# An expert layer whose rows are gathered by selection products and whose weights pass a ring of 19 slots

## What is computed

```python
h = h + swa_sink_attention(rmsnorm(h), ...);  h = h + swiglu(rmsnorm(h), ffn_w_gu, ffn_w_down)
h = h + mamba2_ssd(rmsnorm(h), ...);          h = h + moe_swiglu(rmsnorm(h), w_router, w_gu, w_down)
return rmsnorm(h, ln_final)

def moe_swiglu(h, w_router, w_gu, w_down):
    logits = h @ w_router
    top_v, top_i = lax.top_k(logits, 2)
    gates = softmax(top_v)                       # two gates a token
    for e in range(8):                           # w_gu[e]: 1024 x 7168, w_down[e]: 3584 x 1024
        g, u = split(h @ w_gu[e]);  out += combine[:, e] * ((silu(g) * u) @ w_down[e])
```

## Time and profile before

| | us |
|---|---|
| median of three executions | 1410.24 (1409.48 to 1411.64) |
| profiled execution, its time | 1411.03 |
| profiled execution, its span | 1409.2 |
| attention to router (0 to 561.3) | 561.3 |
| eight expert passes (561.3 to 1395) | 83.7, 118.0, 95.7, 117.1, 97.9, 116.0, 115.3, 90.0 |
| behind the last expert product | 14.2 |

### The profile page before, as it was taken

The page is one execution under the profiler, slowest core; times in us unless marked ns, Lnnn a source line. Parts: engine busy times, 40 slices in busy tenths (PEclk is TensorE's granted clock), DMA queues, the critical chain, the costliest instruction groups (busy, mean ns, idle before and its releaser), DMA issues.

```text
span 1409.2 us, 30487 instructions
## 1 busy us (share of the span) xinstructions
PE 1348.5 (96%) x13282; PEld 806.3 (57%) x13282; DVE 448.3 (32%) x684; ACT 380.0 (27%) x568; POOL 68.9 (5%) x119
## 2 busy tenths in 40 slices
PE   8999999999999999999999988999988999999985
PEld 7778888887999987353344243345233345346342
DVE  7775555447689974101001000000000000000102
ACT  6754444336588843000000000000000001000011
POOL 2043000000002220100000000000000000000000
PEclk9999999999999999999999999999999999999998
DMA  9369855564643448999999999999999999999994
GB/s 352 125 207 413 302 194 179 180 201 128 209 120 122 150 186 335 374 419 425 415 419 424 412 420 424 412 419 424 414 420 425 413 413 424 414 413 412 404 420 184
DMA packets 130491, 463.07 MB, mean 329 GB/s; under 512 B 9600, under 2 KB 35472, under 8 KB 113984
## 3 DMA queue, kind: packets, MB, share of 16 engines
q1 hardware_dynamic: 123808, 440.44, 79.5%
q0 software_dynamic: 4960, 15.95, 2.9%
q10 hardware_dynamic: 1600, 4.82, 1.1%
HBM read 445.06 MB, written 16.12 MB: 327 GB/s over the span
## 4 chain that ended last, share of the span: by engine, by line
PE 64%; issue 12%; SPq 9%; DMA 9%; DVE 3%; POOLq 2%; ACT 1%; DVEq 1%; POOL 0%; ACTq 0%
PE bank L1332 27%; PE bank L1350 11%; SPq L376 9%; PE bank L826 7%; PE bank L828 7%; PE bank L827 7%; DMA e_ring<-moe_w_gu_in 5%; DMA e_ring<-moe_w_down_in 3%; PE bank L1308 2%; POOLq L477 1%; DMA ring<-swa_w_qkv_in 1%; DVE w_lo L1470 1%; PE bank L1323 1%; POOLq L475 0%; PE bank L1048 0%
## 5 line engine op out<-in xcount | busy, mean ns | idle before, releaser
L1332 PE MATMUL bank<-e_ring,xgT 128*32 128x512 f32 (+1 forms) x4800 | 465.3, 540 | 10.6 <-DMA e_ring<-moe_w_gu_in 10.5
L1332 PEld LDWEIGHTS bank<-e_ring,xgT 128*32 128x32 f32 x4800 | 151.3, 110 | 313.1 <-issue 277.4
L1470 DVE TENSOR_TENSOR w_lo<-ring,w_hi 128x2048 fp32r<-128x2048 f32 (+1 forms) x84 | 191.9, 2288 | 108.9 <-ACT w_hi L520 108.6
L520 ACT ACTIVATE w_hi<-ring 128x2048 fp32r<-128x2048 f32 (+1 forms) x84 | 158.9, 1895 | 126.8 <-PE bank L828 118.7
L1350 PE MATMUL bank<-e_ring,m_hT_a 128*32 128x256 f32 x2240 | 133.8, 396 | 14.3 <-DMA e_ring<-moe_w_down_in 14.3
L2027 DVE TENSOR_TENSOR m_hh<-m_sg,bank 128x512 f32<-128x512 f32 (+1 forms) x40 | 22.7, 616 | 376.1 <-PE bank L1332 376.1
L826 PE MATMUL bank<-w_hi,hT_hi 128*128 128x512 f32 (+1 forms) x336 | 130.9, 390 | 2.2 <-DVE w_lo L1470 1.9
L828 PE MATMUL bank<-w_hi,hT_lo 128*128 128x512 f32 (+1 forms) x336 | 129.2, 385 | 0.0
L827 PE MATMUL bank<-w_lo,hT_hi 128*128 128x512 f32 (+1 forms) x336 | 129.2, 384 | 0.0
L1350 PE MATMUL bank<-e_ring,m_hT_b 128*32 128x256 f32 x1920 | 108.2, 380 | 12.8 <-DMA e_ring<-moe_w_down_in 12.8
L1350 PEld LDWEIGHTS bank<-e_ring,m_hT_a 128*32 128x32 f32 x2240 | 76.4, 114 | 68.0 <-issue 23.1
(11 more groups left out here) (362 smaller groups left out, 1357.8 us busy)
## 6 DMA issues: line engine op xcount, KB each, us to landing
e_ring<-moe_w_gu_in SPq DMA_DIRECT2D x120, 1024.0 KB, 22.0
e_ring<-moe_w_gu_in SPq DMA_DIRECT2D x120, 768.0 KB, 21.6
e_ring<-moe_w_down_in SPq DMA_DIRECT2D x88, 1024.0 KB, 18.6
ring<-ffn_w_gu_in SPq DMA_DIRECT2D x28, 1024.0 KB, 6.3
e_ring<-moe_w_down_in SPq DMA_DIRECT2D x32, 512.0 KB, 15.3
ring<-ffn_w_down_in SPq DMA_DIRECT2D x14, 1024.0 KB, 4.9
xg_rows<-zeros POOLq DMA_DIRECT2D x48, 256.0 KB, 16.3
ring<-ssm_w_in_in SPq DMA_DIRECT2D x8, 1024.0 KB, 5.0
```

Source lines behind the costliest of these rows:

```text
L520: act.activation(w_hi[:, m % SPLIT, 0:w], ring[:, m % RING, 0:w], ACT.Copy).then_inc(hi_ready, 1)
L1332: ins = pe.matmul(bank[banks[b]][quad, 0:w], xgT[:, k, rows], e_slot(c)[:, block_n * w:(block_n + 1) * w], start=(k == 0), stop=(k == KD - ...
L1470: dve.tensor_tensor(w_lo[:, m % SPLIT, 0:w], ring[:, m % RING, 0:w], w_hi[:, m % SPLIT, 0:w].bitcast(F32), ALU.subtract).then_inc(lo_ready, 1)
```

## The change

- **Ring.** 19 slots: `e_late` holds two slots where `e_last` was one; `e_top` holds two behind the tensors of the layers, in space gained by setting the scratch that POOL's DMA descriptors use to 2048 bytes a partition. Loads ahead of the experts are 19: two right behind the stream (`c_dt_parts`), two behind `SO0`, one behind `c_y`, six behind `lo_ready`, one behind `c_norm`, six behind `chunk_used`, one behind `r_mm`. Chunks 16, 17 and 18, the additional ones, are of 768 KB.
- **Loads in line.** SP's loop is over rounds; the 365 loads behind the first 19 of a round are written out.
- **Rows.** `xg_rows`, its zeros, the scatter, the row loads, `rows_T`, `spread` and the DVE comparisons of `shares_of` go. `xs` stays resident. In each pass DVE makes `sel` (which token goes to which row of the next pass) and `gated` (the same for the own pass, times the gate) (`selections`, `pass_sel`); PE multiplies `gated` by the identity (`pass_shares`, 4 products) and `xs` by `sel` (`rows_next`, 16 products); DVE copies the former into `shares_T`. PE waits for `rows_ready` before the first pass.
- **Small loads.** `rw` and `dtw` are loaded by ACT (in its early list, before `ahead(2)`) instead of by POOL.
- The rows of pass 0 are gathered 64 wide instead of 96.

```diff
@@ ring
-ERING = 16
-SLOT_OF = (13, 14, 15, 0, 1, 2, 3, 4, 5, 6, 7, 8, 9, 10, 11, 12)
+CONTIGUOUS = 15
+SLOT_OF = (17, 18, 13, 14, 15, 0, 1, 2, 3, 4, 5, 16, 6, 7, 8, 9, 10, 11, 12)
+ERING = len(SLOT_OF)
+SCRATCH = 2048
@@ SP
-            with sp.Fori(0, last) as it:
-                here = sp.value_load(order_i[0:1, bass.ds(it % E, 1)], min_val=0, max_val=E - 1)
-                expert_loads(it, here, ERING, LAYER_CHUNKS)
-                following = sp.value_load(order_i[0:1, bass.ds(it % E + 1, 1)], min_val=0, max_val=E - 1)
-                expert_loads(it + 1, following, 0, ERING)
-            final = sp.value_load(order_i[0:1, E - 1:E], min_val=0, max_val=E - 1)
-            expert_loads(last, final, ERING, LAYER_CHUNKS)
+                for p in range(E):
+                    e = 0 if p == 0 else sp.value_load(order_i[0:1, p:p + 1], min_val=0, max_val=E - 1)
+                    for i in range(max(p * LAYER_CHUNKS, ERING), (p + 1) * LAYER_CHUNKS):
+                        sp.wait_ge(chunk_used, it * ROUND_CHUNKS + (MOE0 + i - ERING + 1))
+                        expert_load(e, i)
@@ POOL
-            pool_e.dma_start(rw[:], moe_w_router[0].rearrange("(k p) e -> p k e", p=P)).then_inc(bc_loaded, 16)
-            pool_e.dma_start(dtw[:], block_of(ssm_w_in[0], 0, KD, C0 + G * N, SH)).then_inc(dtw_loaded, 16)
...
-            for t in range(TT):
-                for i in range(2):
-                    pool_e.indirect_dma_start(xg_rows.rearrange("i p d -> (i p) d"),
-                                              bass.IndirectOffsetOnAxis(slots_i[:, i, t:t + 1], 0),
-                                              xs[:, t], None).then_inc(rows_sent, 16)
@@ ACT
             norm_hi(0, (2, 3))
+            act.dma_start(rw[:], moe_w_router[0].rearrange("(k p) e -> p k e", p=P)).then_inc(dtw_loaded, 16)
+            act.dma_start(dtw, block_of(ssm_w_in[0], 0, KD, C0 + G * N, SH)).then_inc(dtw_loaded, 16)
             ahead(2)
...
-                if p == 0:
-                    act.wait_ge(rows_sent, 16 * 2 * TT)
-                act.dma_start(xg[0:rows], xg_rows[it * E + (p + 1)][0:rows]).then_inc(xg_loaded, 16)
@@ PE
+            pe.wait_ge(rows_ready, TT)
             pe.wait_ge(r_rounds, 1)
...
-                def rows_T():
+                def rows_next():
                     n = rows_of(p + 1)
                     for k in range(KD):
-                        ins = pe.transpose(bank[UP[k // 4]][:, k % 4 * P:k % 4 * P + n], xg[0:n, k * P:(k + 1) * P],
-                                           ident[0:n, 0:n])
+                        if k == 4:
+                            pe.wait_ge(shares_ready, it * E + (p + 1))
+                        for t in range(TT):
+                            ins = pe.matmul(bank[UP[k // 4]][:, k % 4 * CAP:k % 4 * CAP + n], xs[:, t, k * P:(k + 1) * P],
+                                            sel[:, t, 0:n], start=(t == 0), stop=(t == TT - 1))
...
+                def pass_shares():
+                    n = rows_of(p)
+                    for t in range(TT):
+                        for i in range(2):
+                            ins = pe.matmul(bank[UP[1]][0:n, t * P:(t + 1) * P], gated[:, i, t, 0:n], ident[:],
+                                            start=(i == 0), stop=(i == 1))
+                    ins.then_inc(shares_mm, 1)
...
-                pe.wait_ge(xg_loaded, it * (16 * E) + 16 * (p + 1))
+                pe.wait_ge(pass_sel, it * E + (p + 1))
                 hidden_T(1, GATE)
-                rows_T()
+                pass_shares()
+                rows_next()
@@ DVE
+            def selections(p):
+                own, following = rows_of(p), rows_of(p + 1)
+                for i in range(2):
+                    for t in range(TT):
+                        dve.tensor_scalar(gated[:, i, t, 0:own], column[:, 0:own], slots[:, i, t:t + 1],
+                                          gates[:, i, t:t + 1], ALU.is_equal, ALU.mult)
...
+                dve.tensor_scalar(slots[:], slots[:], -float(CAP), None, ALU.add)
+                dve.drain()
+                for t in range(TT):
+                    dve.tensor_scalar(sel[:, t, 0:following], column[:, 0:following], slots[:, 0, t:t + 1], None,
+                                      ALU.is_equal)
...
+            def shares_of(it, p):
+                dve.wait_ge(shares_mm, it * E + (p + 1))
+                for t in range(TT):
+                    ins = dve.tensor_copy(shares_T[0:rows_of(p), t], bank[UP[1]][0:rows_of(p), t * P:(t + 1) * P])
+                ins.then_inc(shares_ready, 1)
...
-                if p > 0:
-                    shares_of(p)
+                selections(p)
+                shares_of(it, p)
```

More of the change, by code:

```diff
@@ L124, in build @@
         GR0, SO0, MOE0 = Z0 + 8, Z0 + 8 + 2 * G, Z0 + 8 + 2 * G + KI // 2
-        assert len(stream) == MOE0 and MOE0 % RING == 0 and LAYER_CHUNKS % ERING == 0 and MOE0 % SPLIT == 0
+        assert len(stream) == MOE0 and MOE0 % RING == 0 and MOE0 % SPLIT == 0
         def phase(**shapes):
@@ L152, in build, with loads_of @@
                     (sem(f"e_loaded{r}"), 0) for r in range(ERING)]
+        def loads_of(r):
+            return len(range(r, ROUND_CHUNKS, ERING))
         def chunk(n, w):
@@ L184, in build @@
         root_table = sb("root_table", [P, 8])
-        zeros = sb("zeros", [P, 512])
+        decay_of = sb("decay_of", [P, 3, P])[:]
         choice = sb("choice", [P, 2, TT, E])
@@ L1311, in rows_back @@
                         ins.then_inc(back_mm, 1)
-                def spread():
-                    pe.wait_ge(diag_ready, it + 1)
-                    for b, diag in ((6, diag_slots), (7, diag_gates)):
-                        ins = pe.matmul(bank[b][:], ones[:], diag.rearrange("p i t n -> p (i t n)"), start=True, stop=True)
-                    ins.then_inc(spread_mm, 1)
                 def hidden_T(s, banks):
```

176 lines of the change are left out of this document (71 added, 105 removed).

## The result

The changed kernel takes 1398.13 us (median of 6 executions, 1397.21 to 1401.33) against 1410.94 of the kernel before beside it: 0.9907 of it, 95% interval 0.9893 to 0.992. It is faster by 0.9%, 12.8 us. Run once more, beside other executions of the kernel before, it had 1398.15 us, 0.9891 of it (0.9868 to 0.9914). The profiled execution took 1397.34 us, its span 1395.6. The forecast was 1397.7.

A forecast was written before the change was run, and what follows sets the result against it. Bound: the weight queue to the end of pass 4, then PE. Queue terms of -12.9 us start pass 5 at 1060.8; PE's 321.7 us end it at 1382.5, 12.5 off 1410.24: 1397.7 us, range 1390 to 1407.

The forecast's parts named there:

- The bound: Experts' passes: the weight queue sets the pace to the end of pass 4, then the later of PE and queue.
- Ring, scatter, row loads: Weight queue up to pass 4: three more chunks ahead -5.6 us, scatter gone -5.5, row loads gone -8.3.
- Start: Ahead of the first pass: PE waits for `xs`, so the experts begin at about 566.4, +5.0 us.
- Clock: First chunk of the experts: an idle stretch of 5 us probably lowers PE's clock, +1.5 us (0 to 3.4).
- The sum at pass 4: Queue at the end of pass 4: start, clock and relief sum to -12.9 us, so pass 5 starts at 1060.8.
- PE's additional work: Each pass: `rows_next` and `pass_shares` come, 8 transposes go, net +3.9 us a pass (2.8 to 7).
- Rival C: Passes 5 to 7: DVE's round trips are not hidden, 1.5 us a pass, +4.5 in all: 1402.2 us; chance 0.13.
- B: All passes: the queue gets faster than 105.5 us a pass and PE alone sets the end: 1387.3 us; chance 0.04.
- E: Whole kernel: no change, the queue gains less than half and PE loses twice as much: 1409 us; chance 0.04.
- A: Last passes: the queue sets the end, new products cheap or hidden in PE's waits: 1392.8 us; chance 0.14.
- D: Loads ahead of the experts: the additional chunks do not get ahead, 5.6 us lost: 1403.3 us; chance 0.08.
- F: Kernel start: POOL's seven small loads do not fit the smaller scratch together, each waits: 1415.9 us; chance 0.05.

The follow-up runs named there:

- the other order: Changed kernel without PE's wait for the scaled rows ahead of the first pass, and passes ordered small, large, small, large, large, small, large, small: 1387.00 us.

## Why the prediction was right, step by step

- **The bound.** Queue to the end of pass 4, PE from there: so it came. 5.0 us of waits for loads are left, all at the end of the queue's part, none in pass 7. The queue's last landing is at 1373.8; 2.4 us behind it (as before, 1392.6 to 1395.0) the queue alone would have ended the products at 1376.2, 5.1 us ahead of PE, where the forecast had 4.9.
- **Ring, scatter, row loads.** 5.6, 5.5 and 8.3 us were taken. The runs gave 5.6 for the ring (the start of pass 5; 5.1 at the end); 5.6 for the scatter at the landings of pass 4; and 6.5 for the four loads of passes 1 to 4, where the sum has 6.4. The first load was not taken out by itself; its 1.9 stays an estimate. That the 64-row price held is luck, as its row showed another dip.
- **Start.** +5.0 taken, 5.4 measured against the first gathering product (9.0 against 3.6). The first expert product was reckoned at 566.4 and came at 566.13, with 0.57 us of that owed to a first part that happened to be shorter, which is within what two executions of one kernel differ.
- **Clock.** Undersized: 1.5 us taken, 2.0 measured twice (5.65 against 3.64 us for two chunks; 81.2 against 79.2 for the pass).
- **The sum at pass 4.** -12.9 taken. The landings moved by -13.4, of which 0.57 are the first part. With the measured terms, 5.4 + 2.0 - 5.6 - 5.6 - 6.5 - 1.9 = -12.2 against -12.8: 0.6 us has no name. Pass 5 began at 1059.26 instead of the 1060.8 forecast.
- **PE's additional work.** 3.9 us a pass taken; large passes went from 116.0 and 115.3 to 119.7 (without the wait) and 119.1, the last from the reckoned 78.7 to 82.7. Rival C falls: no gap between the new products. From pass 5 to the last product it was 321.7 by the forecast and 322.1 in the trace.
- **The queue's price.** 105.5 us a pass was too high: without row loads the landings of passes 1 to 5 are 104.7 us apart. It was worked out as a third of the last three passes, and in these lies a stretch that belongs to no pass: the last pass's weights need 111.2 us. The slip did no harm, since the forecast used differences of the same passes; as a price for the other order it would have.
- **The rate's dips.** The forecast took every dip in the rate for a row load and said that they would go. Those in the early passes did (424 GB/s from 770 to 800). In the last two passes some are left without any row load: 391 GB/s from 1270 to 1300, where loads land after 12 to 15 us, while between 1090 and 1120 they took 21. Few loads on the way go with some of these dips, but are not enough to explain them. Three stretches of the changed kernel:

```profile
740.00:760.00 20.00, 20.00 (x362) 12.44 (x365) 0.00 (x0) 0.38 (x1) 0.00 (x0) 1.00 1.01 426
1270.00:1280.00 10.00, 10.00 (x161) 7.05 (x164) 0.00 (x0) 0.77 (x2) 0.00 (x0) 1.00 0.95 378
1220.00:1230.00 10.00, 10.00 (x117) 3.55 (x112) 1.88 (x3) 0.00 (x0) 0.00 (x0) 1.00 0.98 375
```

The loads of the first and the last took about the same 16 us from issue to landing, and one has the full rate, the other a dip. Nor is it the size of the rows: loads of 1 MB with rows of 8 KB fill the first as well as the second. What makes the dips stays open.
- **The total.** -12.5 taken, -12.8 measured by the medians, -13.1 in the traces from the first gathering product to the last product. The start cost a little more, the queue's part gave a little more.
- **Rivals.** B and E are excluded by the time. A, C and D fell above. F's mechanism exists, one load further on than the changed kernel goes.
- **Small things.** ACT's two issues took 0.40 and 0.60 us; its split of the third chunk began at 13.86 instead of 13.09, the next one, which waits for its load, at 17.10 instead of 17.68. Nothing of it shows later. The zeros, the narrower gathering and SP's written-out loads were taken at 0 and not run by themselves; the first gathering product came at 557.69 before and at 557.12 and 558.72 after, so in the first part they bring no more than two executions differ.

## What to carry to other kernels

Where two resources share a pipeline with a buffer between them, price each by stage and follow the chain: here the same 3.6 us of PE work were worth 3.6 us while PE set the end and next to nothing once the queue did. A wait that is put ahead of a loop "for safety" should stand where the data are first read; this one cost 5.4 us of idle time and 2.0 us of half clock behind it, for PE and, through its first release, for the queue; 6.3 us of that reached the end (5.9 in the trace). When a scratch for descriptors is made smaller, look in the trace for growing gaps between the issues of the engine that fills it, not at the time: the gaps were there with the time unchanged.
